# Mixer of a two-block transformer kernel: chunk masks ahead of the query root, row maximum with its sign turned, inverse seeded on GpSimd, exponential's table loaded at the second turn

## The reference, cut to what matters

```
x = x + 0.5 * swiglu(rms_norm(x))
h = rms_norm(x);  proj = h @ w_in                      # 1024 -> 2944
y_rwkv = rwkv7_mixer(token_shift(proj[:1280]))         # 6 heads of 64, a recurrence over tokens
y_attn = attention_mixer(proj[1280:2432])              # 6 heads of 64, q and k normalised per head
y_conv = conv_mixer(proj[2432:])                       # 256 channels, 31 taps, layer norm, silu
x = x + concat(y_rwkv, y_attn, y_conv) @ w_out
x = x + 0.5 * swiglu(rms_norm(x))
```

## Time and profile before

| | |
|---|---|
| three timed runs | 1388.67 us median (1388.60 to 1388.94) |
| the profiled execution's own time | 1390.21 us |
| its span, first to last instruction | 1388.4 us |
| mean granted TensorE clock | 0.994 |
| PE busy | 1360.5 us (98%) |
| DVE busy | 986.1 us (71%) |
| ACT busy | 738.7 us (53%) |
| POOL busy | 160.5 us (12%) |

### The profile page before, as it was taken

One profiled execution on the slowest core, in us unless ns is written; L12 is line 12 of the kernel. 1 busy time (PEld: TensorE's weight loads), 2 busy tenths in 40 slices (PEclk: granted clock), 3 DMA queues, 4 the chain that ended last, 5 costly groups with the idle time before them and its releaser, 6 DMA issues.

```text
span 1388.4 us, 24919 instructions
## 1 busy us (share of the span) xinstructions
PE 1360.5 (98%) x9761; PEld 1183.0 (85%) x9761; DVE 986.1 (71%) x1328; ACT 738.7 (53%) x1052; POOL 160.5 (12%) x156
## 2 busy tenths in 40 slices
PE   9999999999999999999999999999999999999997
PEld 7888889978888888888888988788888998788885
DVE  6666666676776666766657777786666676898887
ACT  6444467454654445644437656564444444755553
POOL 3000000196000000000000049400000033000000
PEclk9999999998999999999999999999999999999999
DMA  9766265110686536766528220285562953456540
GB/s 338 263 193 198 97 197 157 46 75 2 211 268 194 196 123 211 236 192 198 183 67 282 68 92 4 73 291 185 190 199 95 300 187 115 150 190 212 191 141 31
DMA packets 172532, 230.58 MB, mean 166 GB/s; under 512 B 4687, under 2 KB 153863, under 8 KB 172197
## 3 DMA queue, kind: packets, MB, share of 16 engines
q1 hardware_dynamic: 169968, 223.75, 49.4%
q10 hardware_dynamic: 1877, 5.59, 1.1%
q0 software_dynamic: 608, 0.12, 0.1%
HBM read 228.39 MB, written 2.63 MB: 166 GB/s over the span
## 4 chain that ended last, share of the span: by engine, by line
PE 88%; DVE 6%; ACT 3%; POOL 1%; issue 1%; ACTq 0%; POOLq 0%; DVEq 0%
PE bank L477 35%; PE bank L638 27%; PE bank L642 14%; PE bank L1474 3%; DVE gate_lo L462 1%; PE bank L593 1%; PE bank L921 1%; PE bank L1160 1%; PE bank L1347 1%; PE bank L1299 1%; PE bank L1182 1%; DVE up_lo L462 0%; PE bank L1170 0%; DVE down_lo L462 0%; ACT hT L947 0%
## 5 line engine op out<-in xcount | busy, mean ns | idle before, releaser
L462 DVE TENSOR_TENSOR down_lo<-w_down,down_hi 128x2048 fp32r<-128x2048 f32 x67 | 153.5, 2291 | 97.4 <-ACT down_hi L457 97.4
L638 PE MATMUL bank<-hT,up_hi 128*128 128x512 f32 x880 | 220.8, 393 | 0.0
L717 ACT ACTIVATE work<-bank 128x256 f32<-128x256 f32 x176 | 66.8, 384 | 258.6 <-PE bank L642 258.2
L638 PE MATMUL bank<-hT,gate_hi 128*128 128x512 f32 x800 | 199.8, 392 | 0.0
L457 ACT ACTIVATE down_hi<-w_down 128x2048 fp32r<-128x2048 f32 x67 | 128.3, 1915 | 116.5 <-PE bank L477 115.3
L638 PEld LDWEIGHTS bank<-hT,up_hi 128*128 128x128 f32 x880 | 158.2, 189 | 29.2 <-issue 0.6
L462 DVE TENSOR_TENSOR gate_lo<-w_gate,gate_hi 128x2048 fp32r<-128x2048 f32 x66 | 151.5, 2296 | 36.1 <-ACT gate_hi L457 36.0
L462 DVE TENSOR_TENSOR up_lo<-w_up,up_hi 128x2048 fp32r<-128x2048 f32 x72 | 162.7, 2260 | 16.5 <-ACT up_hi L457 16.5
L638 PEld LDWEIGHTS bank<-hT,gate_hi 128*128 128x128 f32 x800 | 147.0, 188 | 28.4
L477 PE MATMUL bank<-down_hi,ff_hi 128*128 128x512 f32 x400 | 156.2, 391 | 0.0
L477 PE MATMUL bank<-down_lo,ff_hi 128*128 128x512 f32 x400 | 156.2, 391 | 0.0
(11 more groups left out here) (376 smaller groups left out, 2310.8 us busy)
## 6 DMA issues: line engine op xcount, KB each, us to landing
w_up<-in_ffn_w_up_dram SPq DMA_DIRECT2D x44, 1024.0 KB, 5.3
w_down<-in_ffn_w_down_dram SPq DMA_DIRECT2D x44, 1024.0 KB, 5.2
w_gate<-in_ffn_w_gate_dram SPq DMA_DIRECT2D x43, 1024.0 KB, 5.4
w_up<-in_w_in_dram SPq DMA_DIRECT2D x12, 1024.0 KB, 9.7
w_down<-in_w_in_dram SPq DMA_DIRECT2D x11, 1024.0 KB, 6.2
w_gate<-in_w_up_dram SPq DMA_DIRECT2D x11, 1024.0 KB, 5.1
w_up<-in_w_up_dram SPq DMA_DIRECT2D x11, 1024.0 KB, 5.0
w_down<-in_w_down_dram SPq DMA_DIRECT2D x11, 1024.0 KB, 5.1
```

The source lines that it names most:

```text
L462: dve.tensor_tensor(staged[kind][1][:, 0:cols], slot[sl][:, 0:cols], staged[kind][0][:, 0:cols].bitcast(F32), ALU.subtract).then_inc(split ...
L638: pe.matmul(bank[:, :], w[0][:, c, at], hpair[:, :, c, :], start=c == 0, stop=False)
L717: act.activation(to[:, q, j * SEQ:(j + 1) * SEQ], psum[2 * q + j][:, SEQ:], ACT.Copy)\
```

## The change

Six edits, all in the mixer's code:

1. The mask `blk16` (16x16 blocks) becomes `up16`, the strictly upper part of those blocks. `mats_of` now takes `DT` straight out of PSUM with it, once for each side, ahead of the masked copy; the pass over the masked copy is gone.
2. The row maxima are written negated by `tensor_reduce(..., negate=True)`. The negation (line 1205) and the wait between the maxima and it are gone, for all 20 heads of the kernel.
3. On DVE the query root's reciprocal and scaling stand behind `below(0)` and `below(1)`, no longer ahead of them.
4. `INV = DT + identity` is done by POOL, after its tap of lag 10, and no longer by DVE.
5. On ACT a one-element exponential after `turned(3)` loads the table there, and `exps(0)` stands ahead of `copy(11)`.
6. In the chain, `exps(1)` to `exps(5)` stood at i = 0, 4, 8, 12, 16; now they stand at 0, 4, 8, 14, 16. At i = 14 it stands behind that group's copies and `copy(3)`.

```diff
-        "blk16": f(row // 16 == col // 16),
+        "up16": f((row < col) & (row // 16 == col // 16)),
...
-                dve.tensor_reduce(amax[:, h, 0:1], logit_[:, h % 2, 0:P], AX, ALU.max)
-                self.link(dve.tensor_reduce(amax[:, h, 1:2], logit_[:, h % 2, P:3 * P], AX, ALU.max))
-                dve.tensor_scalar(anmax[:, h, :], amax[:, h, :], -1.0, None, ALU.mult).then_inc(S["maxed"], 1)
+                dve.tensor_reduce(anmax[:, h, 0:1], logit_[:, h % 2, 0:P], AX, ALU.max, negate=True)
+                dve.tensor_reduce(anmax[:, h, 1:2], logit_[:, h % 2, P:3 * P], AX, ALU.max, negate=True)\
+                   .then_inc(S["maxed"], 1)
...
             attention = ActAttention(act, logit, probT, BANKS1, 3)
+            act.activation(unused, eps["norm"], ACT.Exp)
+            attention.exps(0)
             copy(11)
-            attention.exps(0)
...
-                if i % 4 == 0 and h + 1 < NH1:
-                    attention.exps(h + 1)
+                if i in (0, 4, 8, 14, 16):
+                    attention.exps((0, 4, 8, 14, 16).index(i) + 1)
...
-            dve.wait_ge(S["qk_root"], 1 + past["qk_root"])
-            link(dve.reciprocal(qkst, qkst))
-            dve.tensor_scalar(qkst[:, 0:12], qkst[:, 0:12], 0.125, None, mult).then_inc(S["qk_inv"], 1)
...
-                    dve.tensor_tensor(mats[:, 4 * g + side:4 * g + 4:2].rearrange("p a b c -> p a (b c)"),
-                                      psum[6 + side][:, :].rearrange("p (a b) -> p a b", a=2), m4, mult)\
-                       .then_inc(S["mats_ready"], 1)
-                dve.wait_ge(S["mats_ready"], 2 * g + 2 + past["mats_ready"])
-                dve.tensor_tensor(chain["DT"][:, 4 * g:4 * g + 4, :], mats[:, 4 * g:4 * g + 4, 0, :], blk, mult)\
-                   .then_inc(S["dt_ready"], 1)
+                    products = psum[6 + side][:, :].rearrange("p (a b) -> p a b", a=2)
+                    ins = dve.tensor_tensor(chain["DT"][:, 4 * g + side:4 * g + 4:2, :], products[:, :, 0:CHUNK], up16, mult)
+                    if side == 1:
+                        ins.then_inc(S["dt_ready"], 1)
+                    dve.tensor_tensor(mats[:, 4 * g + side:4 * g + 4:2].rearrange("p a b c -> p a (b c)"), products, m4,
+                                      mult).then_inc(S["mats_ready"], 1)
 
             below(0)
             below(1)
+            dve.wait_ge(S["qk_root"], 1 + past["qk_root"])
+            link(dve.reciprocal(qkst, qkst))
+            dve.tensor_scalar(qkst[:, 0:12], qkst[:, 0:12], 0.125, None, mult).then_inc(S["qk_inv"], 1)
             mats_of(0)
...
-            dve.wait_ge(S["dt_ready"], 3 + past["dt_ready"])
-            dve.tensor_tensor(chain["INV"], chain["DT"], const("eye64").unsqueeze(1).broadcast_to([P, 12, CHUNK]), add)\
-               .then_inc(S["inv_seed"], 1)
...
+                if lag == SIDE_LAGS[-1] + 1:
+                    pool.wait_ge(S["dt_ready"], 3 + past["dt_ready"])
+                    pool.tensor_tensor(chain["INV"], chain["DT"], const("eye64").unsqueeze(1).broadcast_to([P, 12, CHUNK]),
+                                       add).then_inc(S["inv_seed"], 1)
```

More of the change, by code:

```diff
@@ L367, in build @@
         eps = {n: small[:, 8 + i:9 + i] for i, n in enumerate(("norm", "gn", "ln", "kk"))}
-        amax, anmax, asum, arec = (small[:, 12 + 16 * i:28 + 16 * i].rearrange("p (h t) -> p h t", t=NT)
-                                   for i in range(4))
+        anmax, asum, arec = (small[:, 12 + 16 * i:28 + 16 * i].rearrange("p (h t) -> p h t", t=NT)
+                             for i in range(1, 4))
         unused = small[:, 92:93]
@@ L1884, in dve_mix @@
             link(ins)
-            dve.wait_ge(S["qk_root"], 1 + past["qk_root"])
-            link(dve.reciprocal(qkst, qkst))
-            dve.tensor_scalar(qkst[:, 0:12], qkst[:, 0:12], 0.125, None, mult).then_inc(S["qk_inv"], 1)
             bias1 = const("bias1")
             m4 = const("mask4").unsqueeze(1).broadcast_to([P, 2, 4 * CHUNK])
-            blk = const("blk16").unsqueeze(1).broadcast_to([P, 4, CHUNK])
+            up16 = const("up16").unsqueeze(1).broadcast_to([P, 2, CHUNK])
             attention = DveAttention(dve, lambda h: bias1[:, h * 256:(h + 1) * 256],
```

## The result

The changed kernel takes 1393.28 us (median of 20 runs, 1388.82 to 1395.09), the kernel before in the same comparison 1388.83 (20 runs). The ratio is 1.0026, 95% interval 1.0015 to 1.0038: 4.5 us slower, where 6.7 us faster was forecast.

A forecast was written before the change was run, and what follows sets the result against it. PE, busy 98% of the span, was taken as the bound, leaving only its idle time and low-clock time to win. Early waits 3.6 plus first chain 3.6 minus second chain 0.5 made 6.7 us: 1382.0 us, range 1379.3 to 1386.5.

The forecast's parts named there:

- The early waits: Ahead of the chain, PE's waits of 0.80 us (L1418) and 0.98 us (turn 7) go in each mixer: 3.6 us won.
- The table's load: On ACT after `turned(3)`, the load takes 1.28 us without a drain, and `copy(11)` is not held up.
- The rival that it is held: `copy(11)` held 0.6 to 1.2 us a mixer by load or late maxima: 1383.2 to 1384.4 us; 0.10 with slipped seed.
- The seed: On POOL after tap 10 it takes 1.8 us, is ready before PE wants it, and wins nothing.
- The new waits: In the chain, PE waits 1.0 us at group 17 and about 0.9 at group 19; the chain ends 0.5 us later.
- The negation: Line 1205's removal: priced with the move of `exps(4)` in the chain; in the second block 0, within 0.3 us.
- I take it that it holds: In the chains, PE's clock was assumed to stay at 2.4 GHz behind new waits of 1.0 and 0.9 us.
- The rival "slower": Stalls in groups 17 and 19 grow to about 1.6 us, clock falls in both mixers: 1391.4 us; chance 0.05.
- The gain in the first chain: The first mixer's chain takes 12.35 + 0.5 us instead of 16.43 if the clock holds: 3.6 us won.
- The rival "the clock falls once": Clock falls in one mixer behind groups 17 to 19, or timed runs had no low clock: 1385.3 us; chance 0.18.

The follow-up runs named there:

- f_root_first: c_exps13 with the query root ahead of the six maskings (`below`) again, as in the kernel before: 1383.70 us.
- g_table_late: c_exps13 with `copy(11)` ahead of the table load and `exps(0)` again, and no early load: 1383.60 us.
- a_exps12: The changed kernel with `exps(4)` back at i = 12, all other edits kept: 1383.19 us, ratio to before 0.9961.
- b_exps14: The kernel before with `exps(4)` at i = 14 as its only edit: 1397.04 us, ratio 1.0073.
- d_filled: The changed kernel with six products nobody reads ahead of group 17, in PE's wait: 1385.78 us, ratio 0.9984.
- h_only13: The kernel before with `exps(4)` at i = 13 as its only edit: 1386.20 us, ratio 0.9972.
- e_seed_dve: c_exps13 with the seed of the inverses back on DVE, between `normalise(0)` and `normalise(1)`: 1381.84 us, on another chip than c_exps13.
- j_half_filled: The changed kernel with three products nobody reads ahead of group 17, where d_filled has six: 1386.12 us.
- c_exps13: The changed kernel with `exps(4)` at i = 13, between the copies of groups 13 and 14: 1380.52 us, ratio 0.9948 to before.
- c_again: c_exps13 unchanged, measured once more on another chip: 1381.37 us, ratio 0.9945.
- e_again: e_seed_dve unchanged, measured again on one chip with c_again: 1380.54 us.
- i_negated: c_exps13 with the negation of the row maxima as an instruction of its own again: 1382.51 us.

## Why the prediction was wrong

- **The early waits** (3.6 us): right. 1.93 and 1.91 us by the two chain starts, and each part again by f_root_first and g_table_late. One reading was off without harm: each taking of `DT` has 128 elements a side, not 256, and takes 0.28 us; a `mats_of` takes 1.7 us as read.
- **The table's load**: right, no drain, `copy(11)` not held (it waits 0.63 us more for PE). The rival that it is held falls.
- **The seed**: right at 1.81 us and at no gain. DVE and POOL do stand in each other's way there, in a place where it costs nothing.
- **The new waits**: right in place and nearly in size. Group 17's bound was `normalise(4)`'s scalings by the earlier trace rows; they took 1.22 and 1.40 us, the long end, and the wait was 1.15 and 1.33 for a forecast of 1.0.
- **The negation**: priced at nothing beyond `exps(4)`; it is worth 1.1 us by the medians beside the better placed exponentials. What it is worth in the changed kernel itself no run shows.
- **The step that failed** is "I take it that it holds". The sum had the first chain gain 3.6 us and the second lose 0.5. In fact the first went on at 1.2 GHz, down to and past L1491 (6.91 us from there to L1562 before, 8.6 after), and gained nothing; the second fell too, 4.23 us by its chain. That is 3.6 and 3.7 us; with 1.7 and 0.5 more behind the chains it makes 9.5 of the 10.8 us by which the profiled time is off. The new wait of group 17 did it: without it the clock holds (a_exps12), with it alone the clock falls in both mixers (b_exps14), and with PE at work in it the clock holds again (d_filled). Why this wait lowers the clock and L921's wait of 1.13 us in the same execution doesn't, the runs leave open.
- The reasoning behind that step was too thin: the earlier trace rows gave me one wait with a fall behind it (1.58 us) and one without (0.79), and I placed 1.0 with the latter. The rival "slower" had the mechanism and nearly the time (1391.4), but a condition, stalls of 1.6 us, that was not needed.
- **The gain in the first chain** was counted in full from a profiled execution with the slow stretch, and taken off the median too. The rival "the clock falls once" named the case that the timed runs of before had no low clock to lose, and set it aside by the 1.54 us between the profiled time and the median. Nearly half of the 81 executions of before are of that kind, so that gain was too large for the median even with the clock held; h_only13, with 2.5 us instead of 4.5, bears this out.
- The rest goes with the slow stretch behind the lora products. It stands in 5 of 14 profiled executions (the changed kernel, a_exps12, b_exps14, e_seed_dve, j_half_filled), 3.4 us long, and costs at most 1.7 us, half its length (an estimate); before, c_exps13, c_again, d_filled, e_again, f_root_first, g_table_late, h_only13 and i_negated have none there. With and without are the same code in e_seed_dve and e_again, so it belongs to the execution and not to the edit. What calls it up I leave open, and so too the wait of L921, 1.13 us in the changed kernel, 0.5 in c_exps13, 0.7 in f_root_first: it seems to go with where the weights' DMA stands, which no run here tests.

## What to carry to other kernels

A wait costs its length and, in a stretch of small products, perhaps the clock behind it: price each new wait of PE there twice, once with the clock held and once with the next 7 to 14 us of work at 1.2 GHz (the lengths seen here), and let the chance stand between the two unless a row from the same kind of work shows a wait of that length passed unharmed. Look at the granted clock of every timed execution before a gain is read off one profile. An instruction that is in the way at one place of a row of work isn't helped by the next place that looks free on its own engine: ask which engine waits for it and what is queued behind that wait. Here the gap to fill was one group earlier, where ACT idled 0.8 us between two pairs of copies. Where a wait can't be removed, products that nobody reads were cheaper here than the slow clock.

## What the runs showed of the hardware

- The clock fell behind single waits of 1.15, 1.20, 1.21, 1.33 and 1.58 us among 64x64 products, and held behind 0.62, 0.79 and 0.96 us, and behind 0.47 with 0.57 two groups later. Length alone doesn't decide: elsewhere the clock held behind 0.98 us (turn 7, before, both mixers), 1.13 us (L921 and L477, the changed kernel) and 1.28 us (L921, d_filled), and in nearly half of the executions of before the mean clock leaves no room for a fall of this length. The stretch at 1.2 GHz lasted 10.2 us before (310.5 to 320.7) and 13.7 and 10.2 in the changed kernel (312.3 to 326.0, 858.5 to 868.7), 6.8 in b_exps14's second mixer (worked out from the windows with shares between 0.50 and 1.00). The Trainium skill, "TensorE: Matmul & The Clock Gate", section "A second HAM failure mode: psum-queue depth-cycling", says that frequent short idling between groups of products makes the clock go up and down; this case's rows agree in kind, but here a single wait of 1.15 us was enough, where the section has frequent ones.
- A fall needs no wait: behind the lora products PE had worked without a gap, and the clock was 0.50 for 3.4 us. In h_only13 the same came at 879.3 us, behind products of L1593 with 6 columns.
- DVE's line 1205 (128x2) took 0.17 us in the five cases in which POOL was idle, and each of those over 0.2 us, up to 0.99, ran beside an instruction of POOL (before).
